# Cached keys between the projection slabs: page loads and scores of both layers in groups of four units, four PSUM banks for scores and four for slabs

## The chip, the core and the metric

The kernel runs on one core of a Trainium2 chip: TensorE (PE in the profile, its weight loads PEld), VectorE (DVE), ScalarE (ACT), GpSimd (POOL), and SyncE (SP), which only issues DMAs here. On-chip memory is SBUF (128 partitions) and PSUM (eight banks of 128 x 512 float32, where TensorE puts its results). The metric is the device time of one launch in microseconds, the median over runs. The kernel before takes 2241.7 us (three runs, 2241.44 to 2243.01).

## The reference, cut to what matters

One inference step of a two-layer decoder over 256 prompt tokens and 8 sample sequences of one new token each. Every sample sequence has 2048 cached tokens in pages of 128, found through a page table. Layer 0 attends to 256 cached tokens that an indexer picks (2 key heads), layer 1 to all of them with a forget bias (4 key heads). Four more heads in each layer attend to 256 memory tokens. Then come an output projection, a layer norm and a mixture of 16 experts. For the cached keys the reference says:

```
# layer 0                                    # layer 1
_, sel = lax.top_k(sc, topk)                 k_all = concat([pool_k[page_table], k_new])
k_sel = pool_k[phys, off]  (or k_new)        cg = cumsum(concat(lf_past, lf_new))
s = einsum('qkgd,qnkd->qkgn', qg, k_sel)     s = einsum('bqkgd,blkd->bkgql', qg, k_all)
s = s - slopes * dist ; softmax ; @ v_sel    s = s + c_q - c_k ; softmax ; @ v_all
```

All is float32. The kernel scores every cached key in both layers and masks the unpicked ones in layer 0.

## The kernel before

Weights, cached pages and memory caches all come through `ring`, six SBUF slots of 128 x 4096 float32 (2 MB, a "unit"). `plan(layer)` is the list of units in the order in which SP issues them; a unit's slot is its number in the list modulo six, and SP waits before each unit until the slot's last user has freed it (`leave` on TensorE, `free` semaphores). SP works the list strictly in order, so a unit that must wait holds up all behind it. A key unit is 16 pages of 128 KB in layer 0 (eight units) and 8 pages of 256 KB in layer 1 (16 units); each page is a DMA of its own. Value units (`v`) are alike.

**Slabs.** The projections run as slabs of 512 output columns. A slab has two weight units, 64 matmuls of 128x128 by 264 tokens (256 for the memory tokens), four banks, and four copies by ScalarE behind it. Slab g takes banks 4*(g%2) onward, so two slabs alternate between the halves of PSUM. `beside(x)`, called after every fourth matmul (x = 0 to 15), slips small work into a slab: the transposes of memory rows (`turn_memory`), of own keys and values for the output (`own_rows`), of the sample queries (`query_blocks`). Order of slabs before: three of queries (q), keys and values (kv, two in layer 1), memory queries (qm), two of memory keys and values (mkv).

**Cached keys.** After all slabs `sample_scores` runs. VectorE first transposes each key unit in 32x32 blocks (`turn_keys`, semaphore `keys_made`), then TensorE multiplies it with padded queries `Qz` (32x32 matmuls, line 925) into banks 0 to 3. In layer 0 a group is four units of four sequences, in layer 1 two units of two sequences. The units of a group are freed at its last matmuls. Behind the groups come the new key, in layer 0 the mask (line 939), the memory keys, the softmax and `attention`, where prompt attention and the cached values of the sample run interleaved.

**VectorE.** In layer 0 it runs `sample_topk` first: 32 rounds of MAX8 and MATCH_REPLACE8 over 8x2049 scores, then the mask, eight `turn_keys`, the products with the new keys and `prompt_topk(0)`. In layer 1: gates, `cached_gates` (a scan over the cached gates), 16 `turn_keys`.

**ScalarE in layer 1** issues the 128 page DMAs of the forget gates itself (`load_lf`, lines 402 to 405 inside `load_pages`; 6 KB each), 32 ahead of each copy of the three q slabs and 32 ahead of that of the first kv slab. It is also the engine that copies slabs and turned memory rows out of PSUM (line 1528 is the copy helper).

Of the kernel before, what the change touches and what calls it, by code (L numbers as in the profile page):

```python
# [67 lines left out]
IK_EARLY = 6  # L68

# [82 lines left out]
class Ring:  # L152
# [7 lines left out]
    def take(self, n_dma=1):  # L160
        s = self.n % RING
        self.n += 1
        before = self.used[s]
        self.full[s] += 16 * n_dma
        self.used[s] += 1
        return s, self.full[s], self.used[s], before


def plan(layer):

    u = []
    if layer == 0:
        u += [("x", 0, 3), ("x", 1, 1), ("x", 2, 1), ("x", 3, 1), ("kiwi", 0, 1)]
        u += [("qi", k, 1) for k in range(2)] + [("ln", 0, 4)] + [("qi", k, 1) for k in range(2, 4)] + [("ik", 0, 16 * (NB - IK_EARLY))]
    else:
        u += [("f", 0, 1)]
    u += [("q", k, 2 if layer == 0 and k == 3 else 1) for k in range(6)]
    if layer == 1:
        u += [("kv", k, 1) for k in range(2)]
    u += [("mem", 0, 1)] + [("kv", 2 * layer + k, 1) for k in range(2)]  # L180
    u += [("qm", k, 1) for k in range(2)] + [("mkv", k, 1) for k in range(4)]
    n = 8 if layer == 0 else 16
    u += [("k", k, 128 // n) for k in range(n)] + [("mk", k, 4) for k in range(2)]
    u += [("v", k, 128 // n) for k in range(n)] + [("mv", k, 4) for k in range(2)]
    u += [("r", 0, 5)] + [("o", k, 1) for k in range(8)]
    return u


def step_kernel(nc, i, o):

    with ExitStack() as ctx:
# [41 lines left out]
        for layer in range(2):  # L233
# [28 lines left out]
            a.KN = a.KTs  # L262
            a.qiT = work[:, 1024:1024 + 8 * T]
# [95 lines left out]
        for layer in range(2):  # L359
# [3 lines left out]
            for name, k, n in plan(layer):  # L363
                at_l[name, k] = r.take(n)
# [42 lines left out]
        def key_unit(layer, u):  # L407
# [3 lines left out]
            return 2 * (u // 4) + u % 2, 8 * (u // 2 % 2), PAGES // 2  # L411

        def key_base(layer):
            return 9 * layer

# [25 lines left out]
        def _(sp):  # L441
# [23 lines left out]
            for layer in range(2):  # L465
# [10 lines left out]
                for name, k, n_dma in plan(layer):  # L476
# [159 lines left out]
        def _(pe):  # L636
# [6 lines left out]
            def release(layer, name, k=0):  # L643

                leave(pe.transpose(B[4 - (name == "mem")][0:32, 0:32], ident[0:32, 0:32], ident[0:32, 0:32]), layer, name, k)
# [22 lines left out]
            def turn_memory(layer, x):  # L668
# [9 lines left out]
            def slab(layer, name, k, src, n_tok, beside=None, ready=None):  # L678

                g = bump("slab")  # L680
                if g > 2:

                    pe.wait_ge(S("slab_copied"), g - 2)
                for half in range(2):
                    u = arrived(pe, layer, name, 2 * k + half)
                    for n in range(32):
# [5 lines left out]
                            mm = pe.matmul(B[4 * (g % 2) + f][:, 0:n_tok],  # L692
# [8 lines left out]
            def natural(src, nh, t, col=T):  # L701

                n = bump("natural")
                if n > 2:
                    pe.wait_ge(S("natural_copied"), n - 2)
                rows = P if t < 2 else NB
                for h in range(nh):
                    mm = pe.transpose(B[n % 2][0:rows, h * P:(h + 1) * P], src[:, h * col + t * P:h * col + t * P + rows], ident)
                mm.then_inc(S("natural_ready"), 1)

            def own_rows(layer, a, x):

                if x == 1:
                    pe.wait_ge(S("slab_copied"), cnt["slab"] - 1)
                    release(layer, "mem")
                if 2 <= x <= 7:
                    t, v = (x - 2) % 3, (x - 2) // 3
                    natural((a.kT, a.vT)[v], a.nk, t)
                if layer == 1 and 9 <= x <= 12:
                    j = x - 9  # L720
                    if j == 0:
                        pe.wait_ge(S("lf_in"), 16 * PAGES * NB)
                    if j >= 2:
                        pe.wait_ge(S("lf_copied"), j - 1)
                    for pg in range(4):
                        mm = pe.transpose(B[2 + j % 2][:, pg * P:(pg + 1) * P], a.LF[:, (4 * j + pg) * P:(4 * j + pg + 1) * P],
# [3 lines left out]
            def memory_rows(layer, a, x):  # L730

                if x == 2:
                    pe.wait_ge(S("slab_copied"), cnt["slab"] - 1)
# [1841 lines left out]
```

## Time and profile before

| what | value |
|---|---|
| median of three runs | 2241.7 us |
| profiled execution | 2249.78 us, span 2248.0 us |
| PE busy | 2126.4 us (95% of the span) |
| DVE, ACT busy | 769.5 us, 387.2 us |
| mean granted TensorE clock | 0.97 |
| DMA | 647.49 MB, mean 288 GB/s |

The program runs in stages, so the averages hide what matters here: layer 0's projections and indexer run to 325 us of the span, its cached keys and attention to 474 us, output projection and experts to 1117 us; layer 1 repeats this with projections to 1361 us, cached keys to 1453 us and attention to 1590 us. A busy share of TensorE of one says only that records follow each other, not that the array is at its peak. A bracket at the end of a timeline row is the idle time before it, with what ended it. A count of matmul records is twice that of the program's matmuls, since each float32 matmul is two records.

### The profile page before, as it was taken

Reading aid. Unit: us, or ns where it says so; the run is one execution under the profiler, and the core shown is the slowest. Engines: PE = TensorE matmul, PEld = TensorE weight load, DVE = VectorE, ACT = ScalarE, POOL = GpSimd, SP = SyncE. Lnnn points to the kernel's source line nnn. Section 1 sums busy time; section 2 is a strip of 40 time slices with the busy share of each in tenths; the row PEclk is TensorE's granted clock in tenths of the full one; section 3 lists DMA queues with packets and bytes.
Section 4 is the critical chain, followed back from the end, with each engine's and each line's share of the span. In section 5 each row is a group of like instructions: output and inputs, shape, how many; then the busy total and the mean of one; then the engine's idle time right before and its main releaser. Section 6 shows DMA issues by size and latency. Waiting matters only on the chain.

```text
span 2248.0 us, 34894 instructions
## 1 busy us (share of the span) xinstructions
PE 2126.4 (95%) x13909; PEld 1321.0 (59%) x13909; DVE 769.5 (34%) x1262; ACT 387.2 (17%) x932; POOL 8.2 (0%) x11
## 2 busy tenths in 40 slices
PE   8999995899999999999899997799999999999999
PEld 7778873578843435353488885445787444443534
DVE  0249966601572222212500044623016622222223
ACT  1221101410330101011310210033104211010112
POOL 0000000000000000000000000000000000000000
PEclk9999997989999999999999999989999999999999
DMA  9743557794359999999945447998742699999994
GB/s 273 229 150 113 197 176 233 207 345 150 113 216 424 414 430 418 428 420 426 375 155 160 167 172 259 372 345 275 251 149 77 275 426 416 427 415 429 414 417 182
DMA packets 213862, 647.49 MB, mean 288 GB/s; under 512 B 55400, under 2 KB 88953, under 8 KB 184161
## 3 DMA queue, kind: packets, MB, share of 16 engines
q1 hardware_dynamic: 180673, 637.39, 73.6%
q10 hardware_dynamic: 33056, 8.27, 1.9%
q8 instruction: 91, 1.49, 0.3%
q14 instruction: 42, 0.34, 0.0%
HBM read 639.62 MB, written 5.96 MB: 287 GB/s over the span
## 4 chain that ended last, share of the span: by engine, by line
PE 80%; DMA 10%; SPq 5%; issue 2%; ACT 1%; DVE 1%; DVEq 0%
PE bank L692 22%; PE bank L1379 14%; PE bank L1178 10%; PE bank L1426 8%; PE bank L1440 6%; DMA ring<-in_w_down 5%; DMA ring<-in_w_up 4%; SPq L405 4%; PE bank L1352 4%; PE bank L925 2%; PE bank L1055 2%; PE bank L1262 1%; PE bank L1036 1%; SPq L402 1%; PE bank L816 1%
## 5 line engine op out<-in xcount | busy, mean ns | idle before, releaser
L1379 PE MATMUL bank<-ring,AT 128*64 128x512 f32 x2048 | 457.3, 596 | 10.8 <-DMA ring<-in_w_up 8.8
L692 PE MATMUL bank<-X,ring 128*128 128x264 f32 x1664 | 385.7, 389 | 6.2 <-ACT X L1777 6.2
L692 PEld LDWEIGHTS bank<-X,ring 128*128 128x128 f32 x1664 | 312.3, 191 | 64.2 <-issue 13.3
L1379 PEld LDWEIGHTS bank<-ring,AT 128*64 128x64 f32 x2048 | 142.4, 137 | 286.4 <-issue 271.4
L1528 ACT ACTIVATE arena<-bank 128x512 f32<-128x512 f32 (+11 forms) x311 | 137.8, 479 | 715.3 <-PE bank L1426 211.3
L1426 PE MATMUL bank<-ring,arena 128*64 128x512 f32 x1024 | 226.5, 598 | 22.3 <-ACT arena L1528 14.7
L2456 DVE TENSOR_TENSOR X<-bank,X 128x264 f32<-128x264 f32 x256 | 110.8, 433 | 367.7 <-PE bank L1440 365.8
L1178 PE MATMUL bank<-AT,ring 128*128 128x264 f32 x1024 | 233.1, 391 | 0.0
L1178 PEld LDWEIGHTS bank<-AT,ring 128*128 128x128 f32 x1024 | 197.1, 193 | 34.3
L1426 PEld LDWEIGHTS bank<-ring,arena 128*64 128x64 f32 x1024 | 76.9, 137 | 161.6 <-issue 158.9
L1528 ACT ACTIVATE AT<-bank 128x512 f32<-128x512 f32 (+3 forms) x176 | 81.9, 489 | 418.8 <-PE bank L1352 194.9
L1440 PE MATMUL bank<-arena 128*128 128x264 f32 x512 | 138.8, 402 | 0.0
L2066 DVE STREAM_TRANSPOSE ring<-ring 128x4096 f32<-128x4096 f32 x24 | 106.3, 4438 | 93.0 <-DMA ring<-in_cache_b_k 64.6
L925 PE MATMUL bank<-ring,arena 32*32 32x256 f32 (+1 forms) x2560 | 85.6, 458 | 51.6 <-DVE ring L2066 32.5
L1440 PEld LDWEIGHTS bank<-arena 128*128 128x128 f32 x512 | 89.0, 189 | 70.0 <-DVE X L2456 46.7
L692 PE MATMUL bank<-AT,ring 128*128 128x256 f32 x512 | 112.0, 379 | 0.0
L692 PEld LDWEIGHTS bank<-AT,ring 128*128 128x128 f32 x512 | 96.8, 190 | 13.2
L925 PEld LDWEIGHTS bank<-ring,arena 32*32 32x32 f32 x2560 | 53.5, 112 | 82.7 <-DVE ring L2066 34.8
L1998 DVE MAX8 arena<-arena 8x8 f32<-8x2049 f32 (+1 forms) x48 | 79.9, 1664 | 42.9 <-ACT arena L1528 41.3
L1352 PE MATMUL bank<-arena 128*128 128x256 bf16 x768 | 89.5, 273 | 0.0
L1352 PEld LDWEIGHTS bank<-arena 128*128 128x128 bf16 x768 | 74.3, 98 | 13.8 <-issue 2.1
L1999 DVE MATCH_REPLACE8 arena<-arena 8x2049 f32<-8x2049 f32 (+1 forms) x48 | 79.1, 1647 | 0.0
(347 smaller groups left out, 1356.7 us busy)
## 6 DMA issues: line engine op xcount, KB each, us to landing
ring<-in_w_gate SPq DMA_DIRECT2D x64, 2048.0 KB, 16.8
ring<-in_w_up SPq DMA_DIRECT2D x48, 2048.0 KB, 15.5
ring<-in_w_down SPq DMA_DIRECT2D x48, 2048.0 KB, 13.2
ring<-in_w_o SPq DMA_DIRECT2D x16, 2048.0 KB, 11.7
ring<-in_w_up SPq DMA_DIRECT2D x32, 1024.0 KB, 7.7
ring<-in_w_down SPq DMA_DIRECT2D x32, 1024.0 KB, 15.7
ring<-in_cache_b_k SPq DMA_DIRECT2D x128, 256.0 KB, 5.2
ring<-in_cache_b_v SPq DMA_DIRECT2D x128, 256.0 KB, 4.7
```

The lines of the kernel that those rows point to most:

```text
L405: eng.dma_start(dst(g + k), cache[bass.ds(page, 1)].rearrange("a p w -> (a p) w")).then_inc(sem, 16)
L692: mm = pe.matmul(B[4 * (g % 2) + f][:, 0:n_tok], u[:, c * 512 + f * P:c * 512 + (f + 1) * P], src[8 * half + c][:, 0:n_tok], start=(half = ...
L925: mm = pe.matmul(B[r][out, 32 * first:32 * (first + per)], a.Qz[kv // 2][rows, at:at + 32], tile[rows, :, kv * P + 32 * d:kv * P + 32 * d ...
L1178: mm = pe.matmul(B[bank0 + f][:, 0:T], u[:, c * 512 + f * P:c * 512 + (f + 1) * P], Ac[8 * half + c], start=(half == 0 and c == 0), stop=( ...
L1352: mm = pe.matmul(B[GATHER_BANKS[q]][:, c * 2 * P:(c + 1) * 2 * P], M.part[t][k][:, at:at + P], M.sel[:, t * 2 * P:(t + 1) * 2 * P], start= ...
L1379: mm = pe.matmul(B[bank][64 * s:64 * s + 64, :], M.xsT[:, at:at + 64], ring[slots[s][0]][:, c * FE:(c + 1) * FE], start=(half == 0 and c = ...
L1426: mm = pe.matmul(B[2 + q][64 * s:64 * s + 64, :], M.hT[:, at:at + 64], ring[slots[s][0]][:, j * D + q * 512:j * D + (q + 1) * 512], start= ...
L1440: pe.matmul(B[2 + c % 4][:, 0:T], M.ys[:, c * P:(c + 1) * P], M.gt[a], start=True, stop=True).then_inc(sm("scattered"), 1)
L1528: return act.activation(out, in_, ACT.Copy, scale=scale)
L1998: link(dve.max(m8, sc))
L2066: dve.transpose(t[:, :], t[:, :]).then_inc(S("keys_made"), 1)
L2456: dve.tensor_tensor(Xc[c], B[2 + c % 4][:, 0:T], Xc[c], ALU.add).then_inc(sm("scatter_added"), 1)
```

## The change

1. `plan` gives key units places between the weight units, and can put a unit into a named slot. Layer 0: three key units stand behind the kv weights, the fourth behind qm's first half, two behind mkv's first slab, two behind its second. Layer 1: four key units each behind kv, qm, mkv's first and second slab; the slab of values (kv 1) is moved ahead of the third q slab, the slab of keys (kv 0) behind it.
2. The scores are made in `key_products(layer, a, group)`, one group of four units at a time, between the slabs: in layer 0 after qm and after mkv, in layer 1 after kv 0, qm and each of the mkv slabs. In layer 1 a group now has four sequences and twice the matmuls of a group before (`key_unit`).
3. Scores stay in four banks (0 to 3 in layer 0, 4 to 7 in layer 1, `key_banks`); the slabs, transposes and attention items around them use the other four, so slabs no longer alternate once the queries are blocked.
4. VectorE turns key units between the rounds of the sample's top-k (after rounds 10, 12, 15, 18, 26, 28) in layer 0, and four units before `cached_gates` in layer 1. `prompt_topk(0)` goes ahead of `new_keys`.
5. The output rows of the memory keys and values (and layer 1's own keys) are transposed after the last group (`late_rows`); ScalarE gives `memory_done` before those copies.
6. In layer 1 ScalarE's program has the third batch of 32 gate DMAs ahead of the copies of the turned memory rows, and the fourth behind the slab of values.

The diff, cut to its core (lines of ScalarE and VectorE that only take other banks are left out):

```diff
+TURNS_AFTER = [10, 12, 15, 18, 26, 28]
...
-    def take(self, n_dma=1):
+    def take(self, n_dma=1, slot=None):
+        if slot is not None:
+            self.n += (slot - self.n) % RING
...
+        u += units("q", range(3)) + units("q", [3], 2) + units("q", range(4, 6))
+        u += units("mem", [0]) + units("kv", range(2))
+        u += units("k", range(3), 16) + units("qm", [0], 1, 0) + units("k", [3], 16, 5) + units("qm", [1], 1, 1)
+        u += units("mkv", range(2), 1, 0) + units("k", range(4, 6), 16) + units("mkv", range(2, 4), 1, 0)
+        u += units("k", range(6, 8), 16, 4) + units("mk", range(2), 4)
+        u += units("v", range(8), 16) + units("mv", range(2), 4)
     else:
+        u = units("f", [0]) + units("q", range(4)) + units("kv", range(2, 4)) + units("mem", [0])
+        u += units("q", range(4, 6)) + units("kv", range(2)) + units("k", range(4), 8)
+        u += units("qm", range(2)) + units("k", range(4, 8), 8)
+        u += units("mkv", range(2)) + units("k", range(8, 12), 8)
+        u += units("mkv", range(2, 4)) + units("k", range(12, 16), 8) + units("mk", range(2), 4)
+        u += units("v", range(16), 8) + units("mv", range(2), 4)
...
+            def key_products(layer, a, group):
+                per = UNIT // a.W
+                bank = key_banks(layer)
+                us = range(4 * group, 4 * group + 4)
+                if group == 0:
+                    pe.wait_ge(S("q_padded"), (8, 25)[layer])
+                    if layer == 1:
+                        pe.wait_ge(S("lf_copied"), 4)
+                pe.wait_ge(S("keys_made"), key_base(layer) + us[-1] + 1)
...
+                    slab(layer, "q", 1, Xc, T, 4, lambda x: gate_rows(a, x))
                     pe.wait_ge(S("lf_nat"), 3)
                     pe.wait_ge(S("lf_rows_copied"), 1)
-                    slab(layer, "q", 2, Xc, T)
...
+                    slab(layer, "kv", 1, Xc, T, 0, lambda x: turn_memory(layer, x))
+                    slab(layer, "q", 2, Xc, T, 4, lambda x: own_rows(layer, a, x, (a.vT,)))
...
+                    slab(layer, "kv", 0, Xc, T, 0, gates_and_blocks)
+                    key_products(layer, a, 0)
+                    slab(layer, "qm", 0, Xc, T, 0)
+                    key_products(layer, a, 1)
+                    slab(layer, "mkv", 0, Ac, SEQ, 0)
+                    key_products(layer, a, 2)
+                    slab(layer, "mkv", 1, Ac, SEQ, 0)
+                    key_products(layer, a, 3)
+                late_rows(layer, a)
...
+                    load_lf(range(0, 2))
+                    queries(0, 0)
+                    gate_rows(a)
+                    load_lf(range(2, 4))
+                    queries(1, 4)
+                    load_lf(range(4, 6))
+                    turn_rows(Ac, 4)
+                    slab(layer, "kv", 1, heads(a.vT, 4), T, 0)
+                    load_lf(range(6, NB))
```

What stands in a row on TensorE in layer 0 around the end of the slabs, in the program before (L692 a slab's matmuls, L708 own or memory rows, L925 cached keys; `x127` is a count):

```order
L692 MATMUL bank<-AT,ring 128x256 x16
L692 MATMUL bank<-AT,ring 128x256 [waits full1_l0]
L692 MATMUL bank<-AT,ring 128x256 x31
L708 MATMUL bank<-consts,AT 128x128 [waits natural_copied,slab_copied]
...
L925 MATMUL bank<-ring,arena 32x512 [waits keys_made,natural_copied]
L925 MATMUL bank<-ring,arena 32x512 x127
L925 MATMUL bank<-ring,arena 32x512 [waits keys_made]
L946 MATMUL bank<-consts,AT 128x1 [waits keys_made]
```

and in the changed one (L714 slab, L762 query blocks, L944 cached keys, L730 rows):

```order
L762 MATMUL bank<-arena,consts 32x96 [waits natural_copied]
L762 MATMUL bank<-arena,consts 32x96 x15
L714 MATMUL bank<-X,ring 128x264 x20
L944 MATMUL bank<-ring,arena 32x512 [waits keys_made,q_padded]
L944 MATMUL bank<-ring,arena 32x512 x127
L714 MATMUL bank<-AT,ring 128x256 [waits full0_l0,slab_copied]
...
L714 MATMUL bank<-AT,ring 128x256 [waits full1_l0]
L714 MATMUL bank<-AT,ring 128x256 x31
L944 MATMUL bank<-ring,arena 32x512 [waits keys_made]
L944 MATMUL bank<-ring,arena 32x512 x127
L730 MATMUL bank<-consts,arena 128x128 [waits natural_copied,slab_copied]
```

The first group has moved ahead of both mkv slabs, the second stays behind them, and the memory rows that stood inside the last slabs now follow it.

TensorE in layer 1, changed program, where the slab of values begins (L668 transposes memory rows into the banks that the q slab ahead of it has filled):

```order
L714 MATMUL bank<-X,ring 128x264 [waits slab_copied,full2_l1,lf_rows_copied,lf_nat]
L714 MATMUL bank<-X,ring 128x264 x7
L668 MATMUL bank<-consts,ring 128x128 [waits rows_copied,full4_l1,slab_copied]
L668 MATMUL bank<-consts,ring 128x128
L668 MATMUL bank<-consts,ring 128x128 [waits rows_copied]
...
L714 MATMUL bank<-X,ring 128x264 x4
L668 MATMUL bank<-consts,ring 128x128 [waits rows_copied]
```

The slab with the memory rows now follows the second q slab directly; before, a q slab and a kv slab without such transposes stood between them.

ScalarE in the same place (L1528 copies; 32 gate DMAs, of which the last row stands here), in the program before:

```order
L1528 ACTIVATE arena<-bank 128x264 [waits free1_l1]
L1528 ACTIVATE arena<-bank 128x264 x3
L402 TENSOR_LOAD ptab
...
L405 DMA arena<-in_cache_b_lf 128x12
L1528 ACTIVATE arena<-bank 128x264 [waits free3_l1]
L1528 ACTIVATE arena<-bank 128x264 x3
L1528 ACTIVATE AT<-bank 128x256 [waits rows_turned] x16
```

and in the changed one (L1567 copies; the first row is the copy of the second q slab):

```order
L1567 ACTIVATE arena<-bank 128x264 [waits free1_l1]
L1567 ACTIVATE arena<-bank 128x264 x3
L410 TENSOR_LOAD ptab
...
L413 DMA arena<-in_cache_b_lf 128x12
L1567 ACTIVATE AT<-bank 128x256 [waits rows_turned] x16
L1567 ACTIVATE arena<-bank 128x264 [waits free3_l1]
```

In the changed program 32 gate DMAs, the third batch, stand between the copy of the second q slab and the copies of the turned memory rows. Before, all four batches were issued by then, and the last one stood between the copies of the third q slab and of the first kv slab.

## Rows read from the trace of the kernel before

**Rows 1.** Windows: busy us of each engine, PE clock, DMA share, GB/s
```profile
core 0: us, PE busy (x) PEld busy (x) DVE busy (x) ACT busy (x) POOL busy (x), PEclk, DMA share, GB/s
336.00:360.00 24.00, 0.54 (x16) 0.29 (x32) 13.87 (x6) 0.00 (x0) 0.00 (x0) 0.56 0.78 253
1475.00:1590.00 115.00, 114.54 (x670) 60.42 (x670) 32.69 (x93) 35.65 (x118) 0.00 (x0) 0.87 0.85 295
```
**Rows 2.** Timeline of PE, layer 0: start, us, line, form, count [idle before]
```profile
144.03 62.57 PE L692 MATMUL bank<-X,ring 128*128 128x264 f32 x280
...
323.59 1.09 PE L708 MATMUL bank<-consts,AT 128*128 128x128 f32 x8 [1.30 <-ACT AT L1528]
325.48 8.69 PE L925 MATMUL bank<-ring,arena 32*32 32x512 f32 x256 [0.80 <-ACT arena L1528]
359.46 10.15 PE L925 MATMUL bank<-ring,arena 32*32 32x512 f32 x256 [25.29 <-DVE ring L2066]
```
**Rows 3.** Timeline of DVE, layer 0: first and last row of both top-k
```profile
144.40 2.28 DVE L1998 MAX8 arena<-arena 8x8 f32<-8x2049 f32 x1 [41.28 <-ACT arena L1528]
...
292.38 2.27 DVE L1999 MATCH_REPLACE8 arena<-arena 8x2049 f32<-8x2049 f32 x1
...
360.40 0.42 DVE L2029 TENSOR_TENSOR arena<-arena,consts 128x256 f32<-128x256 f32 x1
...
369.06 0.42 DVE L2032 TENSOR_TENSOR arena<-arena,consts 128x256 f32<-128x256 f32 x1
```
**Rows 4.** Timeline of SP's DMA queue, layer 0: keys, then values
```profile
251.61 101.54 SPq L405 DMA_DIRECT2D ring<-in_cache_a_k  x128
...
369.57 79.76 SPq L405 DMA_DIRECT2D ring<-in_cache_a_v  x128
```
**Rows 5.** The chain that ended last, at the last values of layer 0
```profile
449.00 3.06 DMA ring<-in_cache_a_v
```
**Rows 6.** Timeline of ACT and its DMA queue, layer 1: gate pages, slab copies
```profile
1176.33 19.43 ACTq L405 DMA_DIRECT2D arena<-in_cache_b_lf  x32
1195.81 0.95 ACT L1528 ACTIVATE arena<-bank 128x264 f32<-128x264 f32 x3 [21.50 <-issue]
...
1197.14 17.79 ACTq L405 DMA_DIRECT2D arena<-in_cache_b_lf  x31
```
**Rows 7.** Timeline of PE, layer 1: slabs, then the first memory rows
```profile
1173.89 66.13 PE L692 MATMUL bank<-X,ring 128*128 128x264 f32 x296
1239.86 0.60 PE L652 MATMUL bank<-consts,ring 128*128 128x128 f32 x4
```
**Rows 8.** Timeline of PE, layer 1: cached keys
```profile
1370.18 11.84 PE L925 MATMUL bank<-ring,arena 32*32 32x256 f32 x384 [2.90 <-issue]
...
1433.16 3.69 PE L925 MATMUL bank<-ring,arena 32*32 32x256 f32 x128 [1.10 <-issue]
1439.67 3.69 PE L925 MATMUL bank<-ring,arena 32*32 32x256 f32 x128 [2.82 <-issue]
...
1453.33 0.38 PE L946 MATMUL bank<-consts,AT 128*128 128x1 f32 x2
```
**Rows 9.** DMA queues in 1360:1455 (packets, MB, share)
```profile
q1 hardware_dynamic: 16767, 30.78, 90.9%
q8 instruction: 16, 0.26, 1.1%
```
**Rows 10.** Windows of one and of 26 us, layer 1's cached keys
```profile
1374.00:1375.00 1.00, 1.00 (x48) 0.77 (x40) 1.00 (x1) 0.00 (x0) 0.00 (x0) 1.00 0.00 0
...
1427.00:1453.00 26.00, 18.09 (x584) 12.21 (x588) 11.73 (x12) 0.00 (x0) 0.00 (x0) 0.93 1.00 359
```
**Rows 11.** Timeline of DVE, layer 1: key units at full DMA load
```profile
1402.21 4.45 DVE L2066 STREAM_TRANSPOSE ring<-ring 128x4096 f32<-128x4096 f32 x1 [0.96 <-DMA ring<-in_cache_b_k]
1407.59 4.45 DVE L2066 STREAM_TRANSPOSE ring<-ring 128x4096 f32<-128x4096 f32 x1 [0.93 <-DMA ring<-in_cache_b_k]
```
**Rows 12.** Timeline of SP's DMA queue, layer 1: values
```profile
1442.76 99.01 SPq L405 DMA_DIRECT2D ring<-in_cache_b_v  x128
```

More of the change, by code:

```diff
@@ L362, in step_kernel @@
             at_l = {}
-            for name, k, n in plan(layer):
-                at_l[name, k] = r.take(n)
+            for name, k, n, slot in plan(layer):
+                at_l[name, k] = r.take(n, slot)
             units.append(at_l)
@@ L475, in _ @@
                     waited = set()
-                for name, k, n_dma in plan(layer):
+                for name, k, n_dma, _ in plan(layer):
                     s, _, _, before = units[layer][name, k]
@@ L759, in indexer, with late_rows @@
+            def late_rows(layer, a):
+                pe.wait_ge(S("slab_copied"), cnt["slab"])
+                at = other_banks(layer)
+                if layer == 1:
+                    for t in range(3):
+                        natural(a.kT, a.nk, t, at)
+                for src in (a.memK, a.mvT):
+                    for t in range(2):
+                        natural(src, HM, t, at, SEQ)
+                pe.wait_ge(S("natural_copied"), cnt["natural"])
             def indexer(a):
@@ L934, in cached_mask @@
+            def sample_scores(layer, a):
+                bank, other = key_banks(layer), other_banks(layer)
                 def cached_mask(a):
@@ L989, in attention @@
                 per = UNIT // a.W
+                bank, other = key_banks(layer), other_banks(layer)
                 def scores(n):
@@ L1491, in _, with own @@
                     indexer(a)
-                    for k in range(1, 3):
-                        slab(layer, "q", k, Xc, T)
+                    slab(layer, "q", 1, Xc, T, 0)
+                    slab(layer, "q", 2, Xc, T, 4)
+                    slab(layer, "kv", 0, Xc, T, 0, lambda x: turn_memory(layer, x))
+                    def own(x):
+                        own_rows(layer, a, x, (a.kT, a.vT))
+                        if x == 10:
+                            query_blocks(layer, a)
+                    slab(layer, "qm", 0, Xc, T, 4, own)
@@ L1675, in sample_scores @@
                 base = layer * KM_STEPS
+                bank, other = key_banks(layer), other_banks(layer)
                 pad_memory_queries(layer, a)
@@ L1695, in attention @@
                 nm, rs = a.st[:, 0:6], a.st[:, 6:12]
+                bank, other = key_banks(layer), other_banks(layer)
                 def ov_copy(x):
@@ L1954, in _ @@
[L1954 to L1961 removed]
+                        copy(a.S[:, 512 * j:512 * j + 512], B[6 + j % 2][:, :]).then_inc(S("lf_copied"), 1)
@@ new lines, in _ @@
+                    pad_queries(layer, a)
+                    slab(layer, "kv", 0, heads(a.kT, 4), T, 0)
+                    slab(layer, "qm", 0, heads(a.qmT, 4), T, 0, SCALE)
+                late = other_banks(layer)
+                slab(layer, "mkv", 0, heads(a.memK, 4, SEQ), SEQ, late)
+                slab(layer, "mkv", 1, heads(a.mvT, 4, SEQ), SEQ, late)
+                act.sem_inc(S("memory_done"), 1)
+                if layer == 1:
+                    key_rows(late)
+                natural([(P, MN[:, 0, :]), (P, MN[:, 1, :])], 512, late)
@@ L2084, in sample_softmax @@
                 nm, rs = a.st[:, 8:10], a.st[:, 10:12]
+                bank, other = key_banks(layer), other_banks(layer)
                 S_ = a.S[:, 0:L1]
```

320 lines of the change are left out of this document (149 added, 171 removed).

## The prediction

> **What bounds the kernel now.** I read the page's busy shares first, and they say little: PE is busy almost everywhere, so a change has to be read in its own stages. Then the timelines of PE, VectorE, ScalarE and SP's DMA queue around the two stretches of cached keys, the windows for the clock and the DMA load, and the chain of waits for what ends each stage.
>
> Layer 0: TensorE finishes its slabs at 323.6 us, scores the first four key units in 8.69 us and then stands still 25.29 us until VectorE has turned the last four [rows 2]. VectorE turns a unit in 4.45 us [rows 11] but is in the sample's top-k until 294.7 [rows 3], and only then do slots come free: SP needs 101.54 us for 128 key pages, of which some 80 us is issuing (128 value pages without a wait take 79.76 us, 0.62 us each [rows 4]). The stage is not over there: value pages begin at 369.57 and end at 449.3, and the chain goes through the last of them [rows 4, 5]. So layer 0's attention ends with SP's issue of values, and that begins when the last key group frees its slots. What counts in layer 0 is when the last group ends.
>
> Layer 1: the cached keys end at 1453.33 [rows 8], 92 us behind the last slab, with the data queue at 90.9% [rows 9]. Attention behind it has PE busy 114.54 of 115 us [rows 1]: it is bound by TensorE and moves as a whole with the end of the keys, while value pages (from 1442.76 [rows 12]) are ahead of it.
>
> **Layer 0, step by step.** A slab is 128 of the x280 records of [rows 2], 128 x 0.2235 = 28.6 us; with 8 pairs of memory chunks (0.43 to 0.60 each [rows 7]) some 32, with own rows and query blocks 31. From 146.0 (end of q 0): q1 to 174.5, q2 to 203.0, kv to 235, qm to 266. SP can issue key units when q's slots come free: unit 0 at 174.6 to 184.6, unit 1 at 189, unit 2 at 203, unit 3 behind the memory unit at 226 to 236. VectorE's rounds cost (294.65 - 144.40)/32 = 4.70 us each [rows 3]; ten rounds end at 191.3, so unit 0 is there, and the four transposes end at 195.8, 209.6, 228.2 and 246.7, none after a wait. Group 0 thus starts at 266 and takes 8.7: 274.9. mkv's slabs follow; they share one set of banks, so the second waits for the first one's copies, which costs the 1.30 us that a like wait shows [rows 2]; they end near 331.8. Units 4, 5 are issued from 274.9 to 294.8, units 6, 7 (after mkv's third and fourth weights) from 303.3 to 323.1. VectorE: 32 rounds and six transposes from 144.4, plus 2.6 us wait for unit 4, plus the mask of 1.2, end at 325.2; the last two units end at 334.1. Group 1 runs from 334.1 to 342.8, 8.7 instead of 10.15, since it doesn't follow a stand of 25 us (clock 0.56 in it [rows 1]). VectorE's prompt top-k (9.1 us [rows 3]) and the new keys end by 344.4, under the transposes of the late rows on TensorE, some 4 us.
>
> Value pages therefore start at 342.9 instead of 369.57, 26.7 us earlier, and end as much earlier, since SP issues them without a wait. TensorE's own work up to attention gains 369.5 - 342.8 - 4, some 22.7; it waited for value pages in attention, so the later of the two decides, and that is SP. Layer 0: **-26.5 us**. Bounds: -20 if an attention not bound by SP also loses 3 us somewhere, -28 if nothing waits.
>
> **Layer 1, first part: a new wait.** ScalarE issues the gate pages: 32 take 19.43 us from 1176.33, and the copy of the second q slab comes only then, at 1195.81, 16 us after the slab has ended at 1179.3 (24 of the x296 records after 1173.89 [rows 6, 7]). Before, nobody cared, because the next slab had other banks. Now the slab of values with the memory rows is next. Its second beside step transposes into the banks of the q slab, so TensorE waits from 1182.9 to 1197.1; and the fifth chunk needs ScalarE's copy of the first, which stands behind the third batch of 32 gate DMAs (31 of them 17.79 us, to 1214.9 [rows 6]). So TensorE waits again from some 1202 to 1215.5. Queued behind it is everything of layer 1. The slab, begun at 1179.4, has 8 of its 32 us done by then, and ends at 1215.5 + 24 + 1.7 (half clock at first after a stand) = 1241.2 instead of 1211.4: **29.8 us lost**. The fourth batch (18 us) lies under the q slab that follows and costs nothing.
>
> **Layer 1, second part.** q2 with three transposes takes 29.9 (to 1271.0), kv 0 with gates and query blocks 31.1: group 0 can start at 1302.1. Its units came meanwhile (32 pages x 0.62 = 20 us, the last slot free at 1271.0, turned by 1283.6), and `cached_gates` (6 us) is through. Then three times: a group of d us, and until the next group the longer of two: a slab (28.6, or 27.9 with 256 columns), or four key units: 20 us of issue, or 21.6 at the 5.4 us per unit that full DMA load allows [rows 11], 3 us to land and 4.45 to turn, 28 to 29. They are nearly equal; I take 28.9. The last group ends at 1302.1 + 4d + 86.7. Late rows cost 6.7 there (seven transposes of 0.5, with ScalarE's seven copies and two stores behind them). Next step at 1395.5 + 4d, against 1453.3.
>
> What is d? A group has 512 records of 256 columns; no row shows it. The nearest: layer 0's group, the same columns in 256 records, 8.69 us [rows 2]; layer 1's groups of two units, 128 records in 3.69 us, which is 14.8 for 512 [rows 8]. And there is a wait by the name "issue" of 2.5 to 2.9 us between blocks of 128 records, with one packet of the instruction queue for about every 128 records (16 for 2048 [rows 9]). It stands where the data queue is full (share 1.00, period 6.2 to 6.5 us) and is absent through 384 records where DMA was idle at times (share 0.00 at 1374) [rows 8, 10]. So a block costs the longer of its run and its fetch, and the fetch grows with DMA load. Each new group overlaps one 2 MB load, a light to middling load. Low end 8.7, high end 4 x 6.3 = 25; I take **15**, nearest to the blocks at light load (11.84 for three of four). Then layer 1's next step is at 1455.5: **+2.2 us**. Value pages start 6 us later than before, 6.7 + some 23 us ahead of attention instead of 33; attention takes 4.8 us per unit and SP 5, with six slots, so they stay hidden.
>
> The Trainium skill, "Runtime: NRT & Kernel Launch", section on instruction fetch mechanics, says that engines fetch instructions in 16 KiB blocks by DMA and that crossing a boundary is mostly hidden. The trace agrees on the block (0.26 MB in 16 packets) and not on the hiding, by the gaps of 2.5 to 2.9 us. By that rule a group would cost 9 to 10, the second rival.
>
> **Sum.** 2249.8 (profiled execution) - 26.5 + 2.2 = 2225.5. The profiled execution lies 8.1 above the median; -24.3 on 2241.7 gives **2217.4**.
>
> **Rivals.** (1) As forecast. (2) The groups of layer 1 run at the columns' pace, d = 9: for it, layer 0's group shows no gap in 256 records; against it, the gaps of layer 1. 4 x 6 = 24 us less: 2193. (3) The new wait on ScalarE is not there or small, because the gate DMAs issue faster than before: against it, all three batches of the trace take 17.8 to 19.4. 29.8 less: 2188. (4) Slower: instruction fetch. If every block of layer 1's groups costs 6.3 us and each group, its stream starting cold, one more, d = 31: 64 us more than with 15, in sum +40, 2281. It decides for slower from d = 22.5 (+30 against -24.3 and the bound of 4.5); d = 22.5 itself gives 2247. For it: the gaps at full load, and the 2 MB loads that now fall on the groups. Against it: three blocks without a gap at light load. (5) Layer 0's gain is half: units 6 and 7 or mkv's third weights arrive late, or attention has another limit once values come early. For it: VectorE's last transposes already end 2 us behind the slabs. -13 instead of -26.5: 2231. (6) The change doesn't do what it says, groups not overlapping loads: excluded nearly, since the slots free as computed.
>
> **How the numbers follow.** Forecast 0.47, (2) 0.2, (3) 0.06, (4) 0.07, (5) 0.15, (6) and the like 0.05. The forecast's own range by d from 12 to 19 and layer 0 from -28 to -20 is 2204 to 2240. Taking in (2), and leaving out (3) and (4), the range is 2192 to 2240. A measurement of this kernel tells about 0.2%, 4.5 us, from no change: slower by more is (4) and a part of (6), 0.08; within it, the near end of (4) and a part of (5) and (6), 0.08; faster 0.84.
>
> **What would show it.** Layer 0: no stand of 25 us ahead of the second group, value pages from about 343. Layer 1: two waits of TensorE of about 14 us each in the slab of values, near 1183 and 1202 less 26.5, released by ScalarE; four groups of about 15 us with gaps named issue; the first mix slab 24 us earlier. I am wrong if those waits are missing, if the groups take 9 or over 20 us, or if layer 0's attention ends less than 20 us earlier.

## The result, and the profile after

| | before | changed |
|---|---|---|
| median of 7 runs | 2242.8 us (2241.4 to 2247.0) | 2229.9 us (2224.2 to 2236.2) |
| ratio | | 0.9948, 95% interval [0.9932, 0.9965] |
| profiled execution, span | 2249.8, 2248.0 us | 2235.4, 2233.6 us |
| PE busy, mean granted clock | 2126.4 us, 0.970 | 2110.6 us, 0.973 |

The change is faster by 12.9 us, where 24.3 were forecast: the sign is right, the size about half. A repeat later (below) gave 0.9974 [0.9953, 0.9996], so the gain is 5 to 13 us.

Layer 0 after, timeline of PE (start, us, line, form, count, idle before), which answers to [rows 2]; L944 is the scoring of cached keys, L714 a slab:

```profile
266.84 6.48 PE L944 MATMUL bank<-ring,arena 32*32 32x512 f32 x181
274.35 3.22 PE L944 MATMUL bank<-ring,arena 32*32 32x512 f32 x75 [1.03 <-issue]
277.50 27.89 PE L714 MATMUL bank<-AT,ring 128*128 128x256 f32 x128
306.70 27.89 PE L714 MATMUL bank<-AT,ring 128*128 128x256 f32 x128 [1.30 <-ACT arena L1567]
...
335.72 6.47 PE L944 MATMUL bank<-ring,arena 32*32 32x512 f32 x180 [1.12 <-DVE ring L2132]
343.94 3.24 PE L944 MATMUL bank<-ring,arena 32*32 32x512 f32 x76 [1.75 <-issue]
```

The stand of 25.29 us is gone, and both groups are between the slabs. Each takes 10.7 to 11.4 us (266.84 to 277.50, 335.72 to 347.1) and not 8.7. SP's values, against 369.57 and 79.76 in [rows 4]:

```profile
346.92 80.90 SPq L413 DMA_DIRECT2D ring<-in_cache_a_v  x128
```

They end at 427.8 instead of 449.3, 21.5 us earlier. Layer 1's first slab starts at 1096.07 against 1117.00, 20.9 us earlier.

Layer 1 after. First ScalarE and its DMA queue ([rows 6]), then PE in the slab of values:

```profile
1156.66 17.98 ACTq L413 DMA_DIRECT2D arena<-in_cache_b_lf  x32
1174.69 0.95 ACT L1567 ACTIVATE arena<-bank 128x264 f32<-128x264 f32 x3 [20.04 <-issue]
...
1176.00 17.44 ACTq L413 DMA_DIRECT2D arena<-in_cache_b_lf  x31
1193.49 1.97 ACT L1567 ACTIVATE AT<-bank 128x256 f32<-128x256 f32 x6 [17.56 <-issue]
```

```profile
1175.98 1.12 PE L668 MATMUL bank<-consts,ring 128*128 128x128 f32 x4 [12.59 <-ACT arena L1567]
...
1193.92 1.11 PE L668 MATMUL bank<-consts,ring 128*128 128x128 f32 x4 [11.07 <-ACT AT L1567]
```

A window of each stretch behind a wait shows what the waits cost besides (columns as in [rows 1]; the clock is the third figure from the end). The 0.54 and 0.67 are means over both levels: read us by us, the granted clock is 0.50 (1.2 GHz) from 1176 to 1180 and from 1194 to 1197, and 1.00 (2.4 GHz) from 1181 and from 1198 on.

```profile
1175.00:1181.00 6.00, 5.02 (x17) 4.09 (x18) 0.00 (x0) 0.93 (x4) 0.00 (x0) 0.54 0.14 11
1193.00:1200.00 7.00, 6.08 (x24) 5.12 (x25) 0.00 (x0) 2.59 (x8) 0.00 (x0) 0.67 0.05 5
1201.00:1208.00 7.00, 7.00 (x40) 6.00 (x39) 0.00 (x0) 2.25 (x8) 0.00 (x0) 1.00 0.27 75
```

The groups of cached keys of layer 1, first row of each, and the first gap of the first and of the last, answering to [rows 8]; the last two rows are the step behind the cached keys (L946 before, at 1453.33) and the first slab behind attention (1590.97 before):

```profile
1281.20 4.53 PE L944 MATMUL bank<-ring,arena 32*32 32x256 f32 x210
1288.64 6.66 PE L944 MATMUL bank<-ring,arena 32*32 32x256 f32 x256 [2.90 <-issue]
...
1328.06 4.53 PE L944 MATMUL bank<-ring,arena 32*32 32x256 f32 x210 [2.21 <-DVE ring L2132]
...
1375.80 9.19 PE L944 MATMUL bank<-ring,arena 32*32 32x256 f32 x337 [3.88 <-DVE ring L2132]
...
1421.94 5.91 PE L944 MATMUL bank<-ring,arena 32*32 32x256 f32 x209 [3.26 <-DVE ring L2132]
1428.68 2.74 PE L944 MATMUL bank<-ring,arena 32*32 32x256 f32 x128 [0.82 <-issue]
...
1443.58 0.59 PE L965 MATMUL bank<-consts,AT 128*128 128x1 f32 x2 [2.55 <-ACT arena L1567]
...
1579.43 16.13 PE L1194 MATMUL bank<-AT,ring 128*128 128x264 f32 x64
```

Between the groups VectorE turns the four units like this:

```profile
1306.53 4.45 DVE L2132 STREAM_TRANSPOSE ring<-ring 128x4096 f32<-128x4096 f32 x1 [36.90 <-DMA ring<-in_cache_b_k]
1312.70 4.45 DVE L2132 STREAM_TRANSPOSE ring<-ring 128x4096 f32<-128x4096 f32 x1 [1.73 <-DMA ring<-in_cache_b_k]
1318.14 4.45 DVE L2132 STREAM_TRANSPOSE ring<-ring 128x4096 f32<-128x4096 f32 x1 [0.99 <-DMA ring<-in_cache_b_k]
1323.56 4.45 DVE L2132 STREAM_TRANSPOSE ring<-ring 128x4096 f32<-128x4096 f32 x1 [0.98 <-DMA ring<-in_cache_b_k]
```

The two profiles in stages, by those starts: layer 0 up to layer 1's first slab -20.9 us; layer 1 from there to the step behind its keys 347.5 against 336.3, +11.2; attention 135.85 against 137.64, -1.8; the rest -2.9. Sum -14.4, the difference of the spans.

### The profile page after: what moved, and what is told of

The parts are those of the page before. It is cut to its first block, busy times and chain, and to the rows that moved or that the text cites. A ratio compares the mean times of both kernels' runs of the same rounds, so it can differ in the third digit from the quotient of the medians.

```text
span 2233.6 us, 34908 instructions
## 1 busy us (share of the span) xinstructions
PE 2110.6 (94%) x13909; PEld 1315.5 (59%) x13909; DVE 768.9 (34%) x1262; ACT 387.1 (17%) x932; POOL 8.2 (0%) x11
## 4 chain that ended last, share of the span: by engine, by line
PE 74%; DMA 11%; SPq 6%; DVE 3%; issue 3%; ACTq 1%; ACT 1%; DVEq 0%
PE bank L714 15%; PE bank L1395 13%; PE bank L1194 10%; PE bank L1442 8%; DMA ring<-in_w_down 6%; PE bank L1456 6%; SPq L413 4%; DMA ring<-in_w_up 4%; PE bank L1368 4%; PE bank L944 3%; PE bank L1071 2%; DVE ring L2132 1%; ACTq L413 1%; DMA ring<-in_cache_b_k 1%; PE bank L1278 1%
## 5 line engine op out<-in xcount | busy, mean ns | idle before, releaser
L714 PE MATMUL bank<-X,ring 128*128 128x264 f32 x1664 | 390.4, 392 | 6.2 <-ACT X L1818 6.2
L714 PEld LDWEIGHTS bank<-X,ring 128*128 128x128 f32 x1664 | 315.3, 193 | 66.2 <-issue 13.7
L1567 ACT ACTIVATE arena<-bank 128x512 f32<-128x512 f32 (+11 forms) x311 | 137.1, 479 | 793.6 <-PE bank L714 252.0
L1567 ACT ACTIVATE AT<-bank 128x512 f32<-128x512 f32 (+3 forms) x176 | 82.1, 489 | 334.7 <-PE bank L1368 193.0
L714 PE MATMUL bank<-AT,ring 128*128 128x256 f32 x512 | 111.6, 380 | 1.3 <-ACT arena L1567 1.3
L714 PEld LDWEIGHTS bank<-AT,ring 128*128 128x128 f32 x512 | 96.9, 190 | 16.4 <-ACT arena L1567 1.7
L944 PE MATMUL bank<-ring,arena 32*32 32x256 f32 (+1 forms) x2560 | 69.3, 465 | 26.3 <-issue 15.8
L944 PEld LDWEIGHTS bank<-ring,arena 32*32 32x32 f32 x2560 | 44.4, 108 | 49.7 <-issue 27.0
## 6 DMA issues: line engine op xcount, KB each, us to landing
ring<-in_w_gate SPq DMA_DIRECT2D x64, 2048.0 KB, 15.9
ring<-in_w_down SPq DMA_DIRECT2D x32, 1024.0 KB, 15.8
```

Source lines behind the costliest of these rows:

```text
L714: mm = pe.matmul(B[at + f][:, 0:n_tok], u[:, c * 512 + f * P:c * 512 + (f + 1) * P], src[8 * half + c][:, 0:n_tok], start=(half == 0 and c ...
L944: mm = pe.matmul(B[bank + r][out, 32 * first:32 * (first + per)], a.Qz[kv // 2][rows, at:at + 32], tile[rows, :, kv * P + 32 * d:kv * P + ...
L1567: return act.activation(out, in_, ACT.Copy, scale=scale)
```

## The experiments

Each is timed beside the kernel before, and its ratio is to that kernel. The edits are cut to their core. Theory: layer 0 pays by its transposes inside the top-k; layer 1 loses by ScalarE's gate loads ahead of its copies, and by something between the groups. The rivals stand in each expectation.

### Two of the four gate batches to SP

```diff
+ if layer == 1:                       # SP, behind the memory unit
+     for b in range(4, NB): pages(S("lf_in"), b, ..., cache_b_lf, ...)   # sequences 4 to 7
- load_lf(range(4, 6))                 # ScalarE
- load_lf(range(6, NB))
```

> Against the changed kernel, layer 1's last 64 loads of gate pages (sequences 4 to 7) are issued by SP right after the memory unit, and not by ACT between its copies. Theory: the two waits of PE for ACT in the slab of values (12.6 and 11.1 us in the trace of the changed kernel) are the gate pages alone. They go, with the part of the slab that then ran at half clock, so the first group of cached keys starts 22 to 29 us after where it did, counted back: near 1254 instead of 1281 us of the profile, and the whole takes 2230 - 25 = 2205 us (2200 to 2210). Rival: the key pages, which SP now issues 64 instructions later (64 of about 0.6 us, some 36 us), become what the first group waits for, and half or more of the gain is lost: 2218 or more, with a wait of the first key unit on the DMA queue.

Measured: 2220.5 us, 0.9889 [0.9872, 0.9906]; the first group starts at 1266.11 against 1281.20, 15.1 us earlier.

```profile
1174.75 1.12 PE L673 MATMUL bank<-consts,ring 128*128 128x128 f32 x4 [12.91 <-ACT arena L1572]
...
1266.11 4.53 PE L949 MATMUL bank<-ring,arena 32*32 32x256 f32 x210
```

I had expected both waits to go and had moved the wrong loads for that: the first wait ends with the batch of sequences 2 and 3, which ScalarE still issued. The time lies where the rival had it, but not by its cause: no wait for key pages stands ahead of the first group. What the run shows is the price of the second wait. From the end of the first wait to the first group it is 91.4 us against 105.2 (1175.98 to 1281.20) in the changed kernel, 13.9 us less: 11.1 of standing and 2.8 of the lower clock behind it. The other 1.2 of the 15.1 us were there already at the end of the first wait.

### Layer 0's transposes behind the top-k

```diff
-TURNS_AFTER = [10, 12, 15, 18, 26, 28]
+TURNS_AFTER = []
```

> Against the changed kernel, layer 0's six tables of transposes between the rounds of the top-k are empty, so that the key units are turned only when the top-k has ended. All else is the changed kernel. Theory: the groups between the slabs pay in layer 0 only because the transposes were moved up into the top-k. Without that, the first group waits until the top-k is over (about 295 us by the profile of before) and four units are turned (about 314 us) instead of starting at 266.8: layer 0 ends 40 to 47 us later than in the changed kernel, 18 to 26 us later than before, and the whole takes 2270 us (2262 to 2278). Rival: the DVE queue has slack there that I don't see, the waits shift into the later memory slabs and it costs under 15 us: 2245 or less.

Measured: 2274.6 us, 1.0139 [1.0121, 1.0158]. Group 0 of layer 0, then layer 1's first slab (1096.07 in the changed kernel):

```profile
313.80 11.28 PE L944 MATMUL bank<-ring,arena 32*32 32x512 f32 x256 [47.20 <-DVE ring L2132]
...
1142.33 19.61 PE L714 MATMUL bank<-X,ring 128*128 128x264 f32 x80 [6.18 <-ACT X L1818]
```

The wait is 47 us and layer 1 starts 46.3 us later: nothing hides it. Putting the group between slabs without the table of transposes is worse than before by 31 us.

### Layer 1 alone, and layer 0 alone in two ways

```diff
 # layer 1 alone: layer 0's plan and order of before
+TURNS_AFTER = []
+... units("qm", range(2)) + units("mkv", range(4))
+u += units("k", range(8), 16) + ...
+key_products(layer, a, 0); key_products(layer, a, 1)   # behind mkv
 # layer 0 alone: layer 1's plan and slabs of before, then
+for group in range(4): key_products(layer, a, group)       # fours
+for group in range(8): key_products(layer, a, group, 2)    # pairs
```

> Against the changed kernel, layer 0 is as before (both groups of cached keys after the memory slabs, transposes after the top-k); layer 1 is the changed one. Theory from the two profiles: layer 0 gave 21.5 us, layer 1 lost 11.2 us up to its values and got 1.8 + 2.9 us back behind them. So layer 1 alone is slower than before by 6.5 to 11 us: 2243 + 8 = 2251 us (2247 to 2255), and the first groups of layer 1 show the same 15 to 16 us each. Rival, by my forecast: layer 1 lost only 2.2 us and the rest of the miss lies in the profile of one run: 2243 to 2246 us.

> Against the changed kernel, layer 1 runs its slabs in the order of before and then four groups of four cached key units one behind the other; layer 0 is the changed one. Theory: layer 0's gain stays whole (21 to 22 us) and layer 1 is about as before, since the DVE turns a unit of keys in 5.4 us and PE scores it in 3 to 4: 2243 - 21 = 2222 us (2217 to 2227), faster than the changed kernel by 4 to 12 us. Rival: the groups between slabs hid loads and transposes that are now in the open, the last groups wait for keys (each group 9 us of waiting between its end and the next start): 2235 us or more, slower than the changed kernel.

> Layer 0 as in the changed kernel; layer 1 in the order of before (all slabs, then the cached keys) and scored in pairs of units, as before, not in fours. In the run with fours at the end (layer 0 alone) PE waited 57.9 us for three groups' transposes, since a group of four holds its four slots until it ends. Theory: pairs take these waits away again (before had 4.4 + 2.2 + 0.6 us of them), so layer 1 costs what it cost before and the whole is before less layer 0's gain: 2243 - 21.5 = 2222 us (2215 to 2228); that is 8 us faster than the changed kernel, whose layer 1 is then a loss. Rival: the changed order of loads in layer 0 or the bank split costs something in layer 1 too, and layer 0's gain is only what the changed kernel shows as a whole: 2230 us or more.

| | median | ratio to before |
|---|---|---|
| layer 1 alone | 2260.8 us | 1.0084 [1.0065, 1.0103] |
| layer 0 alone, fours at the end | 2257.5 us | 1.0072 [1.0051, 1.0092] |
| layer 0 alone, pairs at the end | 2220.4 us | 0.9892 [0.9866, 0.9919] |

Layer 1 alone is slower than before by 17 us, more than my 6.5 to 11; its profile, 11.1 us above that of before, has 4.6 of them in layer 0 (first slab of layer 1 at 1121.59, against 1117.00) and 6.0 in layer 1. Layer 0 is not quite that of before in it, though my expectation said so: the slabs on one set of banks and the late rows stay, and the value pages start at 372.81 instead of 369.57. So this run overstates what layer 1 costs. Layer 0 alone with the pairs of before gives 20.6 us, three quarters of the forecast of layer 0 and what the profile showed. So layer 1 is a loss in the changed kernel: without it the kernel is 9.5 us faster by the medians (2229.9 and 2220.4) and 12.6 by the ratios.

Fours at the end was a clear miss: 35 us over the theory. PE's waits in it:

```profile
1369.30 6.18 PE L942 MATMUL bank<-ring,arena 32*32 32x256 f32 x209 [19.18 <-DVE ring L2128]
...
1404.98 6.91 PE L942 MATMUL bank<-ring,arena 32*32 32x256 f32 x209 [19.66 <-DVE ring L2128]
...
1439.98 6.58 PE L942 MATMUL bank<-ring,arena 32*32 32x256 f32 x209 [19.02 <-DVE ring L2128]
```

I had counted VectorE's 5.4 us a unit against PE's 4 and forgotten the slots. A group of four holds its four slots to its end, so loads and products can't overlap; pairs can. In the changed kernel the slab between two groups is what covers the loads.

### All gate loads but the first batch to SP

```diff
+ gate_pages(range(2, 4))      # SP, behind the memory unit
+ gate_pages(range(4, 6))      # SP, behind q 4
+ gate_pages(range(6, 8))      # SP, behind q 5
- load_lf(range(2, 4)); load_lf(range(4, 6)); load_lf(range(6, NB))
```

> As the changed kernel, but of layer 1's 128 loads of gate pages the last 96 are issued by SP (32 behind the memory unit, 32 behind each of the last two query units), ACT issues only the first 32. The first run with 64 moved took away the second wait of PE (11.1 us and the half clock behind it: group 0 started 15 us earlier) and left the first, 12.9 us, for the loads of sequences 2 and 3. Theory: now the first goes too, another 15 us: group 0 near 1251 against 1266 us there, no wait of PE for ACT in the slab of values, and 2220.5 - 15 = 2205 us (2200 to 2210). Rival: SP's queue, with 64 us of gate loads in it, is late with the next slab's weights and the keys: a wait for DMA of 5 us or more takes its place and the time stays above 2213.

Measured: 2202.2 us, 0.9809 [0.9781, 0.9837]. SP issues the loads in time that it had stood waiting for slots: its waits to issue weights between 1090 and 1240 sum to 41.1 us, against 114.0 in the changed kernel. No wait for ScalarE stands in the slab of values. Timeline of SP's queue, then PE's first two groups:

```profile
1119.56 23.14 SPq L413 DMA_DIRECT2D arena<-in_cache_b_lf  x32
1142.74 0.43 SPq L479 DMA_DIRECT2D ring<-in_w_in_b  x1
1143.91 18.75 SPq L413 DMA_DIRECT2D arena<-in_cache_b_lf  x32
1162.70 0.42 SPq L479 DMA_DIRECT2D ring<-in_w_in_b  x1
1163.86 19.71 SPq L413 DMA_DIRECT2D arena<-in_cache_b_lf  x32
```

```profile
1251.89 4.53 PE L954 MATMUL bank<-ring,arena 32*32 32x256 f32 x210
...
1298.58 4.53 PE L954 MATMUL bank<-ring,arena 32*32 32x256 f32 x210 [1.89 <-DVE ring L2139]
```

The first group starts at 1251.89 (theory 1251), 29.3 us earlier than in the changed kernel. What both waits cost is read more safely from layer 1's first slab on: up to the first group it is 184.8 to 185.1 us in the four profiled kernels with both waits and 156.1 to 156.7 in the four without, 28.5 us by the means. Against layer 0 alone with pairs it is 18.2 us faster: layer 1's groups between the slabs do pay, once the gate loads are out of ScalarE's way. This is the best version here; the next one and the one in halves (2201.3 and 2205.2 us) can't be told from it.

### What holds the groups apart

With the same base, the key pages issued by two queues:

```diff
+ if layer == 1 and k >= 4: per = per // 2       # SP: pages 0 to 3
+ key_pages(range(4, 8))       # ScalarE: pages 4 to 7, behind kv's copies
```

> As the run before it, and of each key unit of layer 1's groups 1 to 3 SP issues pages 0 to 3 and ACT pages 4 to 7, behind its copies of the slab before. Theory: between two groups PE is held 31 us, of which the slab is 28; the first unit is turned 9.4 us after its slot is free (5 us of issuing 8 loads and 4.4 us of landing) and the last unit's transpose ends 2.2 to 3.9 us after the slab. With half the issuing time on each queue all four are turned some 26 us after the slots are free, under the slab: the three waits on the transposes go (about 9.5 us together, with what clock they cost) and it takes 2196 us (2190 to 2202). Rival: the landing at full load, not the issue, spaces the units, or ACT's issuing delays its copies: the waits stay above 2 us each and the gain over the run before is under 4 us.

Measured: 2201.3 us, 0.982 [0.9793, 0.9847]. The rival held. Each queue issues its half in 10.3 us, and VectorE's rows keep about the distance that they have in the changed kernel:

```profile
1272.17 4.45 DVE L2156 STREAM_TRANSPOSE ring<-ring 128x4096 f32<-128x4096 f32 x1 [36.42 <-DMA ring<-in_cache_b_k]
1277.90 4.45 DVE L2156 STREAM_TRANSPOSE ring<-ring 128x4096 f32<-128x4096 f32 x1 [1.28 <-DMA ring<-in_cache_b_k]
1284.33 4.45 DVE L2156 STREAM_TRANSPOSE ring<-ring 128x4096 f32<-128x4096 f32 x1 [1.99 <-DMA ring<-in_cache_b_k]
1289.74 4.45 DVE L2156 STREAM_TRANSPOSE ring<-ring 128x4096 f32<-128x4096 f32 x1 [0.97 <-DMA ring<-in_cache_b_k]
```

Not the issue but the landing of 2.1 MB a unit spaces them: the 16 DMA engines are full in both kernels (share 1.03 to 1.06 from 1269 to 1290 here). One thing blurs the comparison. SP is free earlier too and issues the next slab's weights at 1277.81, while keys still land; in the base they come behind the keys' issue, at 1287.94. Two runs on the landing:

```diff
 # in halves (last unit of groups 1 to 3)
+dve.wait_ge(S("first_half"), 64 * (u // 4))
+dve.transpose(t[:, 0:h], t[:, 0:h])
+arrived(dve, layer, "k", u); dve.transpose(t[:, h:], t[:, h:])
 # half the pages (units 4 to 15 of layer 1)
+if layer == 1 and k >= 4: per = per // 2
```

> As the kernel with the last 96 gate loads on SP (2202 us), and the last key unit of each of layer 1's groups 1 to 3 is transposed in two halves, the first as soon as its first four pages are there. The split of the issue over two queues left the spacing of the transposes at 5.4 us, so it is the landing of 2.1 MB a unit that spaces them, and only what stands behind the last landing can go. Theory: the last transpose then costs 2.3 us behind the last landing, not 4.45, and each of the three waits (1.9, 3.1, 2.5 us) shrinks by 2.2: about 6 us of waiting less 0.3 of a second start, 2196.5 us (2193 to 2200), with the waits on the transposes at 0 to 1 us each. Rival: PE then starts a group 2 us earlier, but its first block of instructions or the clock takes it back, and it stays within 2 us of 2202.

> As the kernel with the last 96 gate loads on SP (2202 us), but of each key unit of layer 1's groups 1 to 3 only the first half of the pages is loaded (the other half of the slot keeps what was there); transposes and products are all done. Theory: the landing spaces the transposes (5.4 us a unit of 2.1 MB). With 1.05 MB a unit they stand back to back at 4.45 us, the last ends 7 us under the slab, and the three waits (7.5 us together) are gone: the groups start 44 us apart and not 46.7, and it takes 2194 us (2190 to 2197). Rival: the transpose itself or its semaphore path sets the spacing; then it stays 5.4 us and the first wait is only 2 to 3 us shorter than before by the earlier first landing.

Half the pages: 2198.3 us, 0.9807 [0.9788, 0.9827]. This kernel leaves out half of the key pages of units 4 to 15, so it is a probe and no version to use. The four transposes are one run without a gap, and PE has no wait for them:

```profile
1276.50 17.56 DVE L2141 STREAM_TRANSPOSE ring<-ring 128x4096 f32<-128x4096 f32 x4 [33.17 <-DMA ring<-in_cache_b_k]
1321.16 17.43 DVE L2141 STREAM_TRANSPOSE ring<-ring 128x4096 f32<-128x4096 f32 x4 [27.09 <-DMA ring<-in_cache_b_k]
```

```profile
1254.39 4.53 PE L956 MATMUL bank<-ring,arena 32*32 32x256 f32 x210
...
1299.64 4.53 PE L956 MATMUL bank<-ring,arena 32*32 32x256 f32 x210
...
1343.22 4.51 PE L956 MATMUL bank<-ring,arena 32*32 32x256 f32 x209
...
1387.16 4.51 PE L956 MATMUL bank<-ring,arena 32*32 32x256 f32 x209
```

The four starts span 132.8 us, against 139.1 in the base (1251.89 to 1390.98): 6.3 us less. Fewer pages are also issued faster (9.6 us instead of 19.7), so by itself this run could mean either; the split run, with the same 10 us of issue and all the bytes, leaves the landing. The windows 1274:1298 of the base and of this kernel (the last two figures are the DMA share and GB/s) say the same:

```profile
1274.00:1298.00 24.00, 22.69 (x102) 19.02 (x101) 17.26 (x4) 1.24 (x4) 0.00 (x0) 1.00 1.03 380
```

```profile
1274.00:1298.00 24.00, 24.00 (x110) 20.49 (x109) 17.55 (x4) 0.00 (x0) 0.00 (x0) 1.00 0.69 240
```

The time fell by 3.9 us, not the 8 expected, within the spread of both kernels; the mechanism is shown by the rows, not by the time.

In halves: 2205.2 us (2195.5 to 2209.4), 0.983 [0.9807, 0.9852], no gain. The three waits sum to 5.6 us against 7.5. The theory was wrong in its place: when VectorE comes to the last unit, both halves are there, so that it turns them one behind the other; it is the third unit that comes late.

```profile
1283.59 4.45 DVE L2156 STREAM_TRANSPOSE ring<-ring 128x4096 f32<-128x4096 f32 x1 [1.66 <-DMA ring<-in_cache_b_k]
1287.96 2.27 DVE L2151 STREAM_TRANSPOSE ring<-ring 128x2048 f32<-128x2048 f32 x1
1290.15 2.27 DVE L2153 STREAM_TRANSPOSE ring<-ring 128x2048 f32<-128x2048 f32 x1
```

### The changed kernel once more

> The changed kernel once more, beside the others of this call: all of layer 0 and layer 1 as it is. Layer 0's end (the first slab behind the attention) came at 453.1 us in its first profile and at 448.2 to 451.4 in the five other profiled kernels with the same layer 0, so its first profile would stand high by 2 to 3 us. Expected by that: first slab behind the attention of layer 0 near 450.5, both waits of PE for ACT in layer 1 again (12.6 and 11.1 us), and 2229 us (2225 to 2233). Rival: the first result was itself off, and it comes out at 2222 or less (my forecast right) or 2238 or more.

Measured: 2236.1 us (2224.4 to 2241.4), 0.9974 [0.9953, 0.9996], above the 2225 to 2233 expected; both waits for ScalarE again (12.63 and 11.16 us), layer 0's first slab behind attention at 453.98, not 450.5. So the first profile did not stand high. In the nine profiled kernels with this layer 0, layer 1's first slab starts at 1089.5 to 1099.0, mean 1094.5; before had 1117.0. Single profiles of the same code thus lie up to 9.5 us apart by this point, and a difference of a few us between two of them isn't to be read.

## Why the forecast was off

**Layer 0: mechanism right, terms 5.6 us off.** -26.5 forecast, -20.9 in the first profile, -22.5 by the mean of nine, 20.6 by time with layer 1 undone. VectorE's transposes did what the table of rounds said, and SP's values set the end. What failed is "takes 8.7" and "8.7 instead of 10.15": the groups took 10.7 and 11.4. Each has a gap named issue (1.03 and 1.75 us), and its records alone took 9.7, though the clock was 1.00 as in the 8.69 us of before; what slows them no run shows. The second group also waited 1.12 for the last transpose. Value pages started at 346.9, not 342.9, and took 80.9 us. The rival with half the gain (5) fell.

**Layer 1, first part: mechanism right, the exact hit luck.** Two waits in the slab of values, 29.8 us forecast, 28.5 by the kernels without them. Group 0 was forecast at 1302.1; less the 20.9 that layer 1 began earlier that is 1281.2, and it started at 1281.20. But the terms behind it were off both ways: 14.2 and 13.5 us of standing were forecast and 12.6 and 11.1 measured, 4.0 less in all, while the lower clock behind them cost some 4.8 us and not 1.7; and layer 1's first 80 records took 1.3 us longer than before (20.98 and 19.71). Rival (3) fell.

**Layer 1, second part: the step that failed, by the size of two terms.** From group 0's start to the next step 4 x 15 + 3 x 28.9 + 6.7 = 153.4 were forecast; it took 162.4, 9.0 more.
- "They are nearly equal; I take 28.9": the stretches between groups are 30.9, 31.7 and 31.1 us, 7.0 more in all. PE starts a group when the last unit is turned: first transpose 9.2 us after SP could begin to issue, 17.0 us to the last one's start, 4.45 for it, 30.7 in all. My 21.6 + 3 + 4.45 was 1.6 short of that, and the slab of 28 doesn't cover it. With half the bytes the stretches are 28.6, 27.8 and 27.8: slab alone.
- d = 15: the groups took 16.0, 16.0, 15.1 and 15.9, 2.9 more. Rival (2), d = 9, and the slower rival (4), from d = 22.5, fell.
- Late rows 5.8, not 6.7.

Layer 1's +2.2 was +11.2. Layer 0's -26.5 was -20.9. Attention and the rest gave 4.7 back in that profile, which I take for its spread: the stretch from the first slab behind layer 1's attention to the end lasts 652 to 658 us over all the profiled kernels.

What the forecast did not ask is whether layer 1's part pays at all. Its groups save time (86 us from the first product to the last in the kernel with pairs; in the changed one 63 us of products and 9 of waits), and the gate loads on ScalarE take 28.5 away again. Without the waits that part gains 18 us (2220.4 and 2202.2), and with them it costs 10 or more.

Still open: what makes the gap near the 210th record of most groups of layer 1. It was 2.3 to 3.0 us with half the pages loaded and 2.7 to 2.9 in the changed kernel's first two groups, 1.3 or less later in the same group, and all such gaps of the key groups sum to 18.4 us with half the pages and 17.1 in its base; so my "the fetch grows with DMA load" isn't borne out as the cause of this one. Where the group begins at the lower clock the gap shrinks as its first records take longer (1421.94: 5.91 us, then 0.82), so that it ends some 7 us behind the group's start either way (1281.20: 4.53 and 2.90). So what PE waits for there seems to run by its own time from about the group's start. The packets of the instruction queue fit its place, one for about 128 records; that it is the fetch was argued and not tried. The Trainium skill, "Runtime: NRT & Kernel Launch", on instruction fetch mechanics, has such crossings as mostly hidden; if these gaps are such crossings, the trace disagrees, for in the changed kernel they come to 15.8 us.

## What to carry to other kernels

When a stage is moved between others, follow each engine's own program: here 64 loads queued ahead of a few copies on ScalarE took away more than the move gave, and had cost nothing as long as the next slab had other banks. A group that holds all its buffers to its end can't overlap its successor's loads, so that the work between must be longer than the whole chain of last free buffer, landing and transposing; "nearly equal" was a wait all three times here. Time each part of a double change by itself: the halves were -21 and +10 or a little more.

## What the runs showed of the hardware

- Splitting the issue of the same pages over SP and ScalarE halved the issuing (19.7 to 10.3 us for 32 and twice 16 loads) and did not bring the units closer: a transpose of 2.1 MB every 5.4 to 6.9 us, against 5.4 to 6.2, at a DMA share of 1.03 and 380 GB/s in the base.
- A stand of PE of 11 to 13 us was followed by some 4 us at a granted clock of 0.50; the one of 11.1 us cost 13.9 us in all.
- A transpose of half the columns costs half (2.27 against 4.45 us), so that halves are cheap where they help.
- The changed kernel's 13 runs lie 17 us apart (2224.2 to 2241.4), more than the change is worth.
